# A hybrid decoder layer on one core: the first merge slot's branch A and B products placed around the attention's spreads

## What is computed

```python
h = rmsnorm(x, norm_mix_pre[l])
proj = h @ w_in[l]
p_rwkv, p_conv, p_attn, p_gate = jnp.split(proj, IN_SPLITS, axis=-1)
y_a = rwkv7_time_mix(p_rwkv, ...)
y_b = short_conv_mix(p_conv, conv_w[l])
y_c = dilated_attention_mix(p_attn)
g_a, g_b, g_c = jnp.split(jax.nn.sigmoid(p_gate), N_BRANCH, axis=-1)
wb = w_branch[l]
merged = (g_a * (y_a @ wb[:RWKV_WIDTH])
          + g_b * (y_b @ wb[RWKV_WIDTH:RWKV_WIDTH + CONV_WIDTH])
          + g_c * (y_c @ wb[RWKV_WIDTH + CONV_WIDTH:]))
x = x + rmsnorm(merged @ w_out[l], norm_mix_post[l])
```

## Time and profile before

| | |
|---|---|
| median of 3 runs | 1069.0 us (1068.57 to 1069.25) |
| the profiled execution | 1077.28 us, span 1075.5 us |
| mean granted TensorE clock | 0.982 |
| PE busy | 1021.2 us (95% of the span) |
| DVE busy | 524.0 us (49%) |
| ACT busy | 365.1 us (34%) |
| POOL busy | 450.0 us (42%) |

### The profile page before, as it was taken

One profiled execution on the slowest core, in us unless ns is written; L12 is line 12 of the kernel. 1 busy time (PEld: TensorE's weight loads), 2 busy tenths in 40 slices (PEclk: granted clock), 3 DMA queues, 4 the chain that ended last, 5 costly groups with the idle time before them and its releaser, 6 DMA issues.

```text
span 1075.5 us, 15173 instructions
## 1 busy us (share of the span) xinstructions
PE 1021.2 (95%) x6286; PEld 828.1 (77%) x6286; DVE 524.0 (49%) x620; ACT 365.1 (34%) x451; POOL 450.0 (42%) x341
## 2 busy tenths in 40 slices
PE   6998999999999999999898899999999999999996
PEld 5886778777877787778675787787888888888885
DVE  5734742883287338748655564674334242410003
ACT  5422412441244225312462642353423242312122
POOL 3855411541154215332401446336545545454441
PEclk9998999999999999999998899999999999999999
DMA  8232311332133213341800755323333332322221
GB/s 274 79 118 79 113 65 60 97 137 70 52 119 116 80 59 118 118 178 59 309 25 20 254 183 200 106 80 100 95 90 105 85 110 79 116 91 105 83 74 79
DMA packets 107638, 117.75 MB, mean 109 GB/s; under 512 B 2752, under 2 KB 86720, under 8 KB 107584
## 3 DMA queue, kind: packets, MB, share of 16 engines
q1 hardware_dynamic: 99664, 100.70, 29.3%
q10 hardware_dynamic: 7920, 16.25, 3.9%
HBM read 100.70 MB, written 16.25 MB: 109 GB/s over the span
## 4 chain that ended last, share of the span: by engine, by line
PE 60%; issue 15%; DVE 12%; POOL 7%; ACT 4%; DMA 1%; SPq 1%; ACTq 0%; POOLq 0%; DVEq 0%
PE ps L1482 12%; PE ps L1380 12%; PE ps L1382 12%; PE ps L1381 12%; POOL w_lo L531 6%; PE ps L1537 2%; PE ps L1530 2%; DVE sq L1058 1%; DVE xm L1038 1%; DVE xm L1037 1%; DMA w_raw<-w_in 1%; PE ps L1515 1%; PE ps L1566 1%; PE ps L1559 1%; DVE xm L1036 1%
## 5 line engine op out<-in xcount | busy, mean ns | idle before, releaser
L531 POOL TENSOR_TENSOR w_lo<-w_raw,w_hi 128x512 fp32r<-128x512 f32 x296 | 427.6, 1476 | 587.2 <-ACT w_hi L615 586.9
L615 ACT CAST w_hi<-w_raw 128x2048 fp32r<-128x2048 f32 x75 | 143.0, 1907 | 162.2 <-PE ps L1382 144.8
L1380 PE MATMUL ps<-a_hi,w_hi 128*128 128x512 f32 (+1 forms) x416 | 159.2, 383 | 1.3 <-DVE a_lo L1304 1.1
L1482 PE MATMUL ps<-a_hi,w_hi 128*128 128x512 f32 x384 | 158.5, 413 | 0.0
L1381 PE MATMUL ps<-a_lo,w_hi 128*128 128x512 f32 (+1 forms) x416 | 158.5, 381 | 0.0
L1382 PE MATMUL ps<-a_hi,w_lo 128*128 128x512 f32 (+1 forms) x416 | 158.4, 381 | 0.0
L1482 PE MATMUL ps<-a_lo,w_hi 128*128 128x512 f32 x384 | 153.1, 399 | 0.0
L1482 PE MATMUL ps<-a_hi,w_lo 128*128 128x512 f32 x384 | 152.0, 396 | 0.0
L1380 PEld LDWEIGHTS ps<-a_hi,w_hi 128*128 128x128 f32 x416 | 78.2, 188 | 18.0 <-DVE a_lo L1304 1.8
L1381 PEld LDWEIGHTS ps<-a_lo,w_hi 128*128 128x128 f32 x416 | 78.2, 188 | 14.9
L1382 PEld LDWEIGHTS ps<-a_hi,w_lo 128*128 128x128 f32 x416 | 78.2, 188 | 14.9
(11 more groups left out here) (278 smaller groups left out, 1597.9 us busy)
## 6 DMA issues: line engine op xcount, KB each, us to landing
w_raw<-w_in SPq DMA_DIRECT2D x33, 1024.0 KB, 5.1
w_raw<-w_ffn_in SPq DMA_DIRECT2D x44, 512.0 KB, 4.9
spill<-spill_buf ACTq DMA_DIRECT2D x27, 512.0 KB, 2.8
w_raw<-w_ffn_out SPq DMA_DIRECT2D x11, 1024.0 KB, 4.9
w_raw<-w_branch SPq DMA_DIRECT2D x5, 1024.0 KB, 10.1
g_ab<-spill SPq DMA_DIRECT2D x8, 512.0 KB, 5.9
w_raw<-w_out SPq DMA_DIRECT2D x4, 1024.0 KB, 5.0
proj<-spill SPq DMA_DIRECT2D x1, 3072.0 KB, 14.1
```

The costliest lines, as they stand in the source:

```text
L531: g.tensor_tensor(w_lo[:, b, c], w_raw[:, b, c], w_hi[:, b, c].bitcast(F), ALU.subtract).then_inc(lo_ready, 1)
L615: s.copy(w_hi[:, b], w_raw[:, b]).then_inc(hi_ready, 1)
L1380: t_.matmul(dst, w0, a0, start=first, stop=False)
L1482: last = t_.matmul(ps[:, 6 + half], w[:, kt, half * P:(half + 1) * P], a, start=(kt == 0 and step == 0), stop=(kt == KT - 1 and step == 2))
```

## The change

What the engines do is the same; its order, its places and its waits differ.

- The slots are numbered anew: 34 is the first merge slot, 35 the attention part, 36 to 38 the other merge slots.
- The hi and lo of the eight tiles of A and B are made at the start of the attention: on ACT ahead of `keep(0)`, on DVE behind `dilated_bias()`. They get places of their own; the lo of B is written over B's values.
- PE works on 48 projection matmuls behind the statistics, then on two of the sixteen pieces of merge slot 34 (six matmuls), then on the spreads, then on the other fourteen pieces. The last projection tile no longer waits for the copy of the tile before it.
- The attention stage goes by output tile in banks 0 to 3, with a wait for DVE from the fifth tile on. The merge slots use banks 4 to 7 and 0 to 3 in turn; slot 36 waits for all eight gated tiles.
- The attention gate is loaded and its sigmoid taken in two halves; on ACT the first half stands ahead of the hi of y_c. The other gates are loaded once all ten lo are made.
- The first slot of the output product takes token tiles 2, 3, 0, 1.

```diff
-    S_ATT = N_WIN
-    S_MERGE = S_ATT + 1
-    S_OUT = S_MERGE + N_MERGE
+    S_ATT = N_WIN + 1
+    S_MERGE = [N_WIN] + [S_ATT + g for g in range(1, N_MERGE)]
+    S_OUT = N_WIN + N_MERGE + 1
...
+        yb_hi, o = arena("yb_hi", [P, CJ, SEQ], (up32((CONV_T + CJ) * PITCH4) + 511) // 512 * 512, R)
+        yb_lo, _ = arena("yb_lo", [P, CJ, PITCH], CONV_T * PITCH4, R)
+        pt_buf, o = arena("pt_buf", [P, 2, 2 * SEQ], o)
+        ya_hi_last, o = arena("ya_hi_last", [P, 1, SEQ], o, R)
         assert o <= AT_S
+        o_dil, o = arena("o_dil", [P, 2, SEQ], up32(ATT_T * PITCH4))
+        assert o <= (ATT_T + 2) * PITCH4
+        ya_hi_pair = nc.alloc_sbuf_tensor_at("ya_hi_pair", [P, 2, SEQ], R, offset=AT_LORA)
+        ya_hi_next = nc.alloc_sbuf_tensor_at("ya_hi_next", [P, 1, SEQ], R, offset=AT_RUN)
...
+        y_a, _ = arena("y_a", [P, NJ, SEQ], (o + 512 + 511) // 512 * 512)
+        ya_lo, o = arena("ya_lo", [P, NJ, SEQ], (o + 512 + 511) // 512 * 512, R)
+
+        yc_hi, o = arena("yc_hi", [P, 2, SEQ], (AT_C + 511) // 512 * 512, R)
+        yc_lo, o = arena("yc_lo", [P, 2, SEQ], o, R)
+        assert o <= ATT_T * PITCH4
+        g_att, o = arena("g_att", [P, KT, SEQ], up32((ATT_T + 2) * PITCH4))
...
+        merge_bank = lambda g: 4 * ((g + 1) % 2)
...
+            gate = [sd[:, SPILL_GATE + br * KT:SPILL_GATE + (br + 1) * KT] for br in range(3)]
+            load_merge(0)
             par.b = S_ATT % 2
             load(S_ATT, [(half2(par.b), wb[:, 2 * NJ:BT, :])])
...
+            last = (N_WIN - 1 - N_RWKV) % 2
+            sp.wait_ge(pv_done, N_PAIRS)
+            sp.wait_ge(spilled[1 - last], SPILLED[1 - last])
+            sp.wait_ge(spilled[last], SPILLED[last] - 16)
+            sp.dma_start(g_att[:, 0:KT // 2], gate[2][:, 0:KT // 2]).then_inc(g_att_loaded[0], 16)
+            sp.wait_ge(spilled[last], SPILLED[last])
+            sp.dma_start(g_att[:, KT // 2:KT], gate[2][:, KT // 2:KT]).then_inc(g_att_loaded[1], 16)
+            load_merge(1)
+            sp.wait_ge(y_lo_ready, BT)
+            load_gates(0)
+            load_gates(1)
+            for g in range(2, N_MERGE):
+                load_merge(g)
+                sp.wait_ge(pair_merged, g - 1)
+                load_gates(g)
...
+            act.wait_ge(conv_step, 5)
+            act.wait_ge(y_a_ready.sem, NT)
+            for t in range(2 * NJ):
+                s.copy(y_hi(t), y_part(t)).then_inc(y_hi_ready, 1)
             keep(0)
...
+            half = KT // 2
+
+            def gate_att(part):
+
+                act.wait_ge(g_att_loaded[part], 16)
+                c = slice(part * half, part * half + half)
+                s.activation(g_att[:, c], g_att[:, c], ACT.Sigmoid).then_inc(g_att_ready, 1)
...
+            keep(5)
+            gate_att(0)
+            for t in range(2 * NJ, BT):
+                act.wait_ge(y_c_ready, t - 2 * NJ + 1)
+                s.copy(y_hi(t), y_part(t)).then_inc(y_hi_ready, 1)
+            gate_att(1)
+            high(S_MERGE[1], raw_value(S_MERGE[1]), S_MERGE[1] % 2)
             gates(0)
-            high(S_ATT + 2, raw_value(S_ATT + 2), (S_ATT + 2) % 2)
+            high(S_MERGE[2], raw_value(S_MERGE[2]), S_MERGE[2] % 2)
             gates(1)
             for g in range(N_MERGE):
-                high(S_MERGE + g + 2, raw_value(S_MERGE + g + 2), (S_MERGE + g) % 2)
+                if g > 0:
+                    n = S_MERGE[g] + 2
+                    high(n, raw_value(n), n % 2)
...
             dilated_bias()
+            for t in range(2 * NJ):
+                dve.wait_ge(y_hi_ready, t + 1)
+                v.tensor_tensor(y_lo(t), y_part(t), y_hi(t).bitcast(F), ALU.subtract).then_inc(y_lo_ready, 1)
             keep_values(0, 4)
...
+            for t in range(2 * NJ, BT):
+                dve.wait_ge(y_hi_ready, t + 1)
+                v.tensor_tensor(y_lo(t), y_part(t), y_hi(t).bitcast(F), ALU.subtract).then_inc(y_lo_ready, 1)
             for k in range(KT):
+                dve.wait_ge(g_att_ready, 1 + k // 4)
                 if k < KT - 1:
                     dve.wait_ge(att_tile_done, k + 1)
                 else:
                     dve.wait_ge(slot_used, S_ATT + 1)
-                v.tensor_tensor(merged[:, k], ps[:, k], g_att[:, k], ALU.mult).then_inc(att_merged, 1)
...
-                    b0 = 4 * (g % 2) + 2 * br
...
                     if kt == 0 and step == 0:
-                        pe.wait_ge(spill_copied, 2 * NT * PER_T + i - (1 if i < 2 else 0))
                         if i == 2 * N_LEFT - 1:
                             pe.wait_ge(o_ready, N_PAIRS)
+                        else:
+                            pe.wait_ge(spill_copied, 2 * NT * PER_T + i - (1 if i < 2 else 0))
...
-            fill_left(40)
...
+            def merge(g, pieces):
+
+                b = S_MERGE[g] % 2
+                wh = w_hi[:, b].rearrange("p (k c) -> p k c", k=KT)
+                wl = w_lo[:, b].rearrange("p (k c) -> p k c", k=KT)
+                for br, m, k in pieces:
+                    if g == 0 and (br, m, k) == (1, 0, 0):
+                        pe.wait_ge(spill_copied, 2 * (N_WIN - N_RWKV))
+                    c = slice(m * P, (m + 1) * P)
+                    kt = br * NJ + k
+                    if m == 0 and k % 2 == 0:
+                        part_ready(S_MERGE[g], kt // 2)
+                    last = three(ps[:, merge_bank(g) + 2 * br + m], wh[:, kt, c], wl[:, kt, c], y_hi(kt), y_lo(kt), k == 0, k == NJ - 1)
+                return last
+
+            MERGE = [(br, m, k) for br in range(2) for m in range(2) for k in range(NJ)]
+            pe.wait_ge(y_lo_ready, 2 * NJ)
+            merge(0, MERGE[:2])
             pe.wait_ge(dist_ready, 3)
...
-            fill_left(8)
-            pe.wait_ge(spill_copied, 2 * (N_WIN - N_RWKV))
+            merge(0, MERGE[2:]).then_inc(slot_used, 1)
...
+            pe.wait_ge(y_lo_ready, BT)
+            for m in range(KT):
+                c = slice(m * P, (m + 1) * P)
+                if m >= 4:
+                    pe.wait_ge(att_merged, m - 3)
+                for k in range(2):
                     if m % 4 == 0:
                         part_ready(S_ATT, 2 * k + m // 4)
-                    last = three(ps[:, m], wh[:, k, c], wl[:, k, c], y_hi[:, 2 * NJ + k], y_lo[:, 2 * NJ + k], k == 0, k == 1)
-                    if k == 1:
-                        last.then_inc(att_tile_done if m < KT - 1 else slot_used, 1)
...
+                    last = three(ps[:, m % 4], wh[:, k, c], wl[:, k, c], y_hi(2 * NJ + k), y_lo(2 * NJ + k), k == 0, k == 1)
+                last.then_inc(att_tile_done if m < KT - 1 else slot_used, 1)
+            for g in range(1, N_MERGE):
+                if g == 1:
+                    pe.wait_ge(att_merged, KT)
+                else:
                     pe.wait_ge(pair_merged, g - 1)
...
+                merge(g, MERGE).then_inc(slot_used, 1)
...
                 pe.wait_ge(a_lo_ready, NT + m + 1)
-                for t in range(NT):
-                    if m == 0 and t == 2:
+                for t in (2, 3, 0, 1) if m == 0 else range(NT):
+                    if m == 0 and t == 0:
```

More of the change, by code:

```diff
@@ L367, in in_scores, with y_hi, y_lo, y_part @@
             return slice(c, c + P)
-        PART_ORDER = [*range(2 * NJ, BT), *range(2 * NJ)]
+        merge_bank = lambda g: 4 * ((g + 1) % 2)
+        def y_hi(t):
+            if t < NJ:
+                return ya_hi_pair[:, t] if t < 2 else (ya_hi_next, ya_hi_last)[t - 2][:, 0]
+            return yb_hi[:, t - NJ] if t < 2 * NJ else yc_hi[:, t - 2 * NJ]
+        def y_lo(t):
+            if t < NJ:
+                return ya_lo[:, t]
+            return yb_lo[:, t - NJ, PAD:PITCH] if t < 2 * NJ else yc_lo[:, t - 2 * NJ]
+        def y_part(t):
+            return y_a[:, t] if t < NJ else cols(CONV_T + t - NJ)[:, 0] if t < 2 * NJ else y_c[:, t - 2 * NJ]
         top_of = lambda kind, t=slice(0, NT): small[:, 0:NK * NT * HG].rearrange("p (g t h) -> p g t h", g=NK, t=NT)[:, kind, t]
@@ L468, in _, with load_merge, load_gates @@
                              sd[:, SPILL_ATT + which * AJ + 2:SPILL_ATT + (which + 1) * AJ]).then_inc(dil_loaded, 16)
+            def load_merge(g):
+                par.b = S_MERGE[g] % 2
+                load(S_MERGE[g], [(half8(par.b), wb[:, 0:2 * NJ, g * SC:(g + 1) * SC])])
+            def load_gates(g):
+                for br in range(2):
+                    sp.dma_start(g_ab[:, g % 2, br], gate[br][:, 2 * g:2 * g + 2]).then_inc(g_ab_loaded[g % 2], 16)
+            gate = [sd[:, SPILL_GATE + br * KT:SPILL_GATE + (br + 1) * KT] for br in range(3)]
+            load_merge(0)
             par.b = S_ATT % 2
             load(S_ATT, [(half2(par.b), wb[:, 2 * NJ:BT, :])])
[L472 to L487, removed]
+            last = (N_WIN - 1 - N_RWKV) % 2
[13 more added lines that the diff above has]
+                load_gates(g)
             for m in range(N_OUT):
@@ L1243, in _ @@
             dve.wait_ge(y_c_ready, 2)
-            def y_part(t):
```

(12 more changed lines are left out.)

48 lines of the change are left out of this document (11 added, 37 removed).

## The result

The changed kernel is faster by 0.58%: ratio 0.9942, 95% interval 0.9929 to 0.9954. Its six runs have a median of 1064.44 us (1061.06 to 1065.62), the kernel before 1069.12 in as many. The ratio on record is not the quotient of these two medians, which is 0.9956, a gain of 4.7 us. On 1069.0 the ratio gives 1062.8, a gain of 6.2 us; the forecast was 9.1. The sign and the mechanism came as forecast; by the ratio the time lies at the upper edge of the range, by the median 1.4 us beyond it. The profiled execution took 1065.62 us (span 1063.9): 11.7 less than the one before. So the two profiles show about twice what the runs show, and most of this study is about that difference.

What follows compares the result with a forecast made beforehand. PE and its waits were taken to bound the 82.06 us late stretch: 12.1 us less in the new order, minus 3.0 clock loss, gives 9.1; early part 0; 1069.0 - 9.1 = 1059.9 us, range 1056.1 to 1063.0.

Steps and rivals of the forecast that it cites:

- The base: Whole kernel: profiled execution 1077.28 us against a run median of 1069.0, the 8 us taken as the profile's cost.
- the 82.06: Old order's time in us from PE's last projection tiles at 569.73 to the output product at 651.79.
- late stretch: Last projection tiles or statistics to the output product's first matmul; forecast 9.1 us faster, 8.0 to 10.4 likely.
- clock loss: Time lost to TensorE's low clock at the spreads in the new order: bounded 1.7 to 4.1 us, taken as 3.0.
- sum for the new order: Late part after the change: 65.4 matmuls + 3.6 spreads + 1.0 added wait = 70.0 us, before a clock loss of 3.0.
- The new stop: Merge slot behind the attention stage waits for all eight DVE multiplies: 1.0 us lost once.
- The 5.01 us: PE's stand before the attention stage, ending at 595.02; claimed to go, with 3.3 us to spare.
- The early part: Eight hi and eight lo of A and B at the attention's start: cost 0, softmax input 2.3 us late.
- the 3.65 us of slack: First exponential: DVE's input ready at 527.82, ACT began at 531.47; claimed to swallow the 2.3 us delay.
- The clock that doesn't fall: Rival: clock holds on the spreads; gain 12.1 us, time 1056.9, or 1056.1 with the early 0.8; chance 0.12.
- Later waits: Rival: slot 38's cast on ACT behind the third gate pair's sigmoid delays PE; 1061 to 1065 us; chance 0.08.
- The rival with the shifted operand: Rival: B's lo, 8 bytes off, slows 32 merge matmuls; at most 1.1 us plausible, worst 21 us (1081); chance 0.04.

Runs made afterwards that it cites:

- the 29 runs: Runs of the unchanged kernel before, on the same chip as its repeat, beside that repeat's twelve; they lie between 1068.89 and 1077.33 us.
- the second profile: The kernel before profiled once more with no edit: profiled execution 1074.12 us, median of its twelve runs 1070.46 us.
- near relative: The changed kernel with the lo of branch B at the start of its rows and each subtraction of B waiting for the one before: 1064.53 us, ratio 0.9944.
- Undoing the placement: The changed kernel with 40 projection matmuls ahead of the spreads, 8 behind, and all merge slots after the attention stage: 1071.90 us, ratio 1.003.
- taking the cover away: The changed kernel with PE waiting behind the spreads for the lo of y_c before the fourteen merge pieces: 1069.86 us, ratio 0.999.
- the doubled lo: The changed kernel with eight more subtractions, result unused, on DVE behind the eight early ones: 1072.31 us.

## Why the prediction was right, and where it was off

**The base was one draw.** This step failed: "the profile costs 8 us that I take to be the same on both sides", and with it the 82.06 against which the sum was made. The 8 us were the scatter of single executions. Between the two profiles of this kernel, 1077.28 and 1074.12, 2.7 of the 3.2 us lie in the late stretch, where the clock was low for 6.8 us more. For the other 5 us to the median no profile was taken; the mean clock of the 29 runs, 0.982 at 1077.33 and 0.991 at 1068.89, makes low clock likely for them too. Of the 11.7 us between the profiles before and after, 9.4 lie in the late stretch and 1.7 behind it, as much as a low stretch of 3.4 us costs; near 684 the profile before has one, the one after none. I gave the new order's clock loss a range of its own, 1.7 to 4.1, and took the old order's from a single execution. Against the second profile's 79.41, the same sum for the new order gives 79.4 - 73.0 = 6.4 us, and 6.2 were measured. So close a match is luck: that profile was the slowest of its twelve runs.

**The sum for the new order** was 70.0 + 3.0 = 73.0; measured were 72.66 and 74.34. Matmuls and spreads (65.4 + 3.6) and the stop came to 70.95 instead of 70.0; 0.5 of the difference is the shifted lo, which I had bounded by 1.1 and left out, the rest is not explained. The new stop was 1.0 as forecast (from 607.29, the last matmul's start, to 608.53, less one step of 0.23). The clock loss was 1.7 and 3.4, and 0 in one near relative; against these, the 3.0 was a fair value.

**The 5.01 us** went, with the lo of y_c ready at 590.8 under merges that ran to 596.6: 5.8 us of margin where 3.3 were forecast. Undoing the placement and taking the cover away both show that it is nearly all of the gain. One reading of the old order was wrong: the four multiplies that its first merge slot waited for were not long done.

```profile
605.60 4.87 DVE L1258 TENSOR_TENSOR merged<-ps,g_att 128x512 f32<-128x512 f32 x8 [2.00 <-ACT g_att L832]
```

DVE began them only behind the whole attention gate, the fourth ended at 608.09, and the slot started at 608.19, 0.17 us later than in step. In that profile it is no more than this, but it is the stop of 0.58 in the second one, where PE came to the slot sooner.

**The early part** cost nothing that the runs can show, as said, but not with the margin that was said. I forecast the eight lo to end at 525.1; they ended at 525.7 in an execution that was 0.3 ahead. Three of them took 1.67 to 1.77 us each while POOL worked on its slot, and the first maximum came 3.65 us late in place of 2.3. Of the 1.35 more, 0.66 are its last small operation: it took 0.83 us, where before it took 0.17, just as POOL began its next slot (529.88). That is the 3.65 us of slack to the last tenth. With the doubled lo, where this operation took 0.17 again, the first eight had left 0.55 of it. The Trainium skill's rule ("SBUF — State Buffer", section "SBUF: two separate sides"), by which the loser waits for a whole instruction, had given a cost of 0.3; the trace lies between it and my sum: the three began 1.66 us apart, where the rule gives 1.96 and I had 1.25. The median of 1.22 that I had used is a length that none of the four had: two took 1.76 beside POOL and two 0.68 behind its last quarter (which ended at 599.45), so the sentence that those of 1.22 show the rule not paid in full has nothing under it.

**The rivals.** The clock that doesn't fall (0.12) occurred, in an execution of a near relative; it is not another outcome but a part of the scatter, and should have stood in the forecast's own mean. Later waits did not come: slot 38's cast was done at 626.0 and PE took up the slot at 630.7. (The terms of that rival add up to 18.2 us, not 17.3; with the longest landing that is 23.2, just over the 22.8 at which PE needs it.) The rival with the shifted operand had its mechanism right and a price of 0.5 us, inside the bound of 1.1 and far from the 21 of its worst case.

**Left open.** At equal late stretch the medians of single profiles don't order the kernels within 1 us, since low stretches come and go elsewhere too (near 131, 534 and 684). What share the clock has in the 6.2 us of the ratio would take many more profiles. Why the clock falls on the same spreads sometimes early, sometimes late and once not at all, these runs do not show.

## What to carry to other kernels

Before a sum is made against a profile, see where its time stands among the runs: an execution 8 us over the median may be not "the profile's cost" but another draw, and the part that differs (here the length of a low clock) must get the same range on both sides. A chain through two engines that the matmul engine waits for is best covered by work that needs none of its results; look then at which wait this work must pay for its banks. Effects below the scatter (a stop of 0.85, a shifted operand of 0.5) are told by the stretch of the trace and its low clock time, not by the total.

## What the runs showed of the hardware

- The same program has its clock low behind the same spreads for 17.1 or 10.2 us; the changed one for 3.4 or 6.8. Where the four spreads stood in a row, 3.7 us at full clock, it began anywhere from 1.5 us after the first one's start to 1.0 us behind the last one's end, and in one profile not at all. Keeping the four spreads apart by 1.36 us of dense matmuls kept the clock up in every profile taken so (three), at 0.33 us more for each spread.
- An fp32r moving operand that starts 8 bytes off made the steps of its own and the neighbouring matmuls 0.2324 us instead of 0.2267.
- A subtraction on DVE of 0.68 us took 1.67 to 1.77 beside POOL's subtraction of weights, and POOL's, 1.28 alone, took 1.34 to 1.73 beside them.
